# Last normalisation of a two-layer decoder trunk: block 0's second pass as a product with a scaled identity on TensorE, output rows stored in four halves

## The reference

```python
def layer_norm(x, g, b):
    xf = x.astype(jnp.float32)
    mu = jnp.mean(xf, axis=-1, keepdims=True)
    var = jnp.mean(jnp.square(xf - mu), axis=-1, keepdims=True)
    return ((xf - mu) * lax.rsqrt(var + LN_EPS) * g + b).astype(x.dtype)

def reference(...):
    h = layer_norm(x, ln_in_g, ln_in_b)
    for l in range(DEPTH):                      # DEPTH = 2
        mix = hybrid_mixer(h, ...)              # input projection, attention, gating, convolution, output projection
        h = layer_norm(DEEPNORM_ALPHA * h + mix, ln_mix_g[l], ln_mix_b[l])
        ffn = grouped_moe(h, ...)               # 16 experts, top 2 of one group of 4
        h = layer_norm(DEEPNORM_ALPHA * h + ffn, ln_ffn_g[l], ln_ffn_b[l])
    return h
```

## Time and profile before

| what | value |
|---|---|
| median of three runs | 640.27 us |
| the profiled execution | 642.03 us |
| its span, first to last instruction | 640.3 us |
| mean granted TensorE clock | 0.996 of full speed |
| busy share: PE, DVE, ACT, POOL | 97%, 47%, 33%, 23% |
| data moved | 246.70 MB, mean 385 GB/s |

### The profile page before, as it was taken

How to read it: one execution, slowest core, us unless ns; L and a number is a source line. 1 busy time by engine, 2 the same in 40 slices (tenths; PEclk the granted TensorE clock), 3 DMA queues, 4 the chain that set the end, 5 groups by cost and what they waited for, 6 DMA issues and landing times.

```text
span 640.3 us, 8170 instructions
## 1 busy us (share of the span) xinstructions
PE 618.4 (97%) x3239; PEld 335.2 (52%) x3239; DVE 298.5 (47%) x619; ACT 208.1 (33%) x465; POOL 148.7 (23%) x139
## 2 busy tenths in 40 slices
PE   9999999999999999997999999999999999999993
PEld 5887887534344344342488878764344344344331
DVE  6898897122141231230578988851141231330326
ACT  5831963232032131130184368342032131131211
POOL 1999400440000000000049971007000000000000
PEclk9999999999999999999999999999999999999998
DMA  8999299999999999999999646999999999999991
GB/s 358 431 425 415 108 427 360 377 430 427 412 426 428 427 426 427 427 425 429 429 428 381 234 198 272 416 338 416 432 417 426 431 423 428 427 425 423 432 383 69
DMA packets 21785, 246.70 MB, mean 385 GB/s; under 512 B 3276, under 2 KB 3404, under 8 KB 6384
## 3 DMA queue, kind: packets, MB, share of 16 engines
q1 hardware_dynamic: 18576, 236.56, 88.5%
q10 hardware_dynamic: 1152, 5.77, 2.3%
q0 software_dynamic: 2016, 3.82, 1.6%
HBM read 246.51 MB, written 3.15 MB: 390 GB/s over the span
## 4 chain that ended last, share of the span: by engine, by line
PE 80%; DMA 11%; DVE 7%; issue 1%; ACT 1%; DVEq 0%
PE bank L765 28%; PE bank L790 15%; PE bank L651 13%; DMA ring<-in_units 11%; PE bank L816 4%; PE bank L625 4%; PE bank L871 2%; DVE w_split L1470 2%; PE bank L883 2%; PE bank L731 2%; PE bank L698 1%; PE bank L639 1%; PE bank L777 1%; PE bank L953 1%; PE bank L579 1%
## 5 line engine op out<-in xcount | busy, mean ns | idle before, releaser
L765 PE MATMUL bank<-ring,xe_pair 128*64 128x512 f32 x976 | 213.3, 593 | 5.7 <-DMA ring<-in_units 5.7
L765 PEld LDWEIGHTS bank<-ring,xe_pair 128*64 128x64 f32 x976 | 71.3, 137 | 145.0 <-issue 134.0
L790 PE MATMUL bank<-ring,area_b 128*64 128x512 f32 x480 | 107.0, 596 | 1.6 <-DVE area_b L1693 1.6
L1691 DVE TENSOR_TENSOR area_b<-area_b,bank 128x512 f32<-128x512 f32 x16 | 11.0, 688 | 205.9 <-PE bank L765 205.9
L1326 POOL DMA_INDIRECT rows<-normal_rows,tiny_i x14 | 14.4, 1026 | 267.6 <-DVE tiny_i L1643 240.4
L1310 POOL TENSOR_TENSOR in_lo<-ring,in_hi 128x512 fp32r<-128x512 f32 x56 | 72.0, 1334 | 12.2 <-ACT in_hi L1081 12.2
L1158 ACT ACTIVATE area_b<-bank 128x512 f32<-128x512 f32 x16 | 9.6, 597 | 187.3 <-PE bank L765 187.3
L790 PEld LDWEIGHTS bank<-ring,area_b 128*64 128x64 f32 x480 | 32.9, 137 | 66.9 <-issue 59.0
L1136 ACT ACTIVATE xe_pair<-bank,small 128x128 f32<-128x128 f32 x128 | 47.0, 466 | 45.9 <-PE bank L731 35.6
L1277 POOL TENSOR_TENSOR rstd<-var_eps,tiny 128x1 f32<-128x1 f32 x18 | 10.6, 594 | 191.8 <-DVE var_eps L1402 191.8
L1712 DVE SCALAR_TENSOR_TENSOR y_lo<-bank,tiny,y_hi 128x512 fp32r<-128x512 f32 x32 | 24.0, 750 | 59.7 <-ACT y_hi L1171 59.7
(11 more groups left out here) (206 smaller groups left out, 789.4 us busy)
## 6 DMA issues: line engine op xcount, KB each, us to landing
ring<-in_units SPq DMA_DIRECT2D x101, 2048.0 KB, 19.5
ring<-in_units SPq DMA_DIRECT2D x8, 1024.0 KB, 23.0
ln_par<-in_ln_rows ACTq DMA_DIRECT2D x4, 1024.0 KB, 10.5
extra<-in_units SPq DMA_DIRECT2D x2, 2048.0 KB, 13.8
extra<-in_units SPq DMA_DIRECT2D x2, 1536.0 KB, 19.9
expert_half<-in_units SPq DMA_DIRECT2D x2, 1024.0 KB, 8.6
normal_rows<-mix SPq DMA_DIRECT2D x4, 512.0 KB, 8.8
h<-in_x SPq DMA_DIRECT2D x2, 512.0 KB, 4.1
```

What stands on the lines that cost most here:

```text
L765: mm = pe.matmul(bank[2 + m][e * SLOTS:(e + 1) * SLOTS, :], x[:, k, at + e * SLOTS:at + (e + 1) * SLOTS], w[c][:, m, e, :], start=k == 0, ...
L790: mm = pe.matmul(bank[5 + n][e * SLOTS:(e + 1) * SLOTS, :], hidT[:, k, e * SLOTS:(e + 1) * SLOTS], w[:, k, e, :], start=k == 0, stop=k == ...
```

## The change

The second pass of block 0 leaves VectorE. ScalarE makes a 128x128 diagonal matrix, the identity scaled row by row with block 0's `rstd` (`scaled_ident`, in memory that is free by then). TensorE forms, for each half, identity times the shift rows plus that diagonal times the half of the first pass, in banks 5 and 6, in float32. ScalarE copies each bank to `h`, and the copy is what SP waits for. VectorE makes block 0's first pass in two halves and tells TensorE of each; its work on block 1 is as before. SP now stores four halves, in the order block 0 first half, block 1 first half, block 0 second half, block 1 second half. Three semaphores get new names because they now serve both ends (`input_ready` is `rows_centred`, `conv_out` is `rows_out`, `proj_pe` is `block_product`). Of the diff, the places that only rename are left out.

```diff
+        scaled_ident = nc.alloc_sbuf_tensor_at("scaled_ident", [P, P], F32, offset=xT_at)
...
-            sp.wait_ge(result_ready, 1)
-            sp.dma_start(out[0, 0:P, :], h[:, 0, :]).then_inc(out_done, 16)
             for n in range(2):
                 half = slice(n * BANK, (n + 1) * BANK)
-                sp.wait_ge(result_ready, n + 2)
+                sp.wait_ge(rows_out, DEPTH + n + 1)
+                sp.dma_start(out[0, 0:P, half], h[:, 0, half]).then_inc(out_done, 16)
+                sp.wait_ge(result_ready, n + 1)
                 sp.dma_start(out[0, P:2 * P, half], h[:, 1, half]).then_inc(out_done, 16)
-            sp.wait_ge(out_done, 16 * 3)
+            sp.wait_ge(out_done, 16 * 4)
...
+            def result_products():
+
+                pe.wait_ge(par_in, 16 * (2 * DEPTH + 1))
+                for n in range(2):
+                    pe.matmul(bank[5 + n][:, :], ident, ln_par[:, 1, n * BANK:(n + 1) * BANK], start=True, stop=False)
+                pe.wait_ge(rows_kept, TB * DEPTH + 1)
+                for n in range(2):
+                    pe.wait_ge(rows_centred, 2 * TB * DEPTH + n + 1)
+                    pe.matmul(bank[5 + n][:, :], scaled_ident[:, :], h[:, 0, n * BANK:(n + 1) * BANK], start=False, stop=True)\
+                      .then_inc(block_product, 1)
+
             def layers_from(l):
 
                 n = layer(l)
                 if l == DEPTH - 1:
                     with pe.If(n > SLOTS):
                         more_rounds(l)
+                    result_products()
                     return
...
+            last = TB + DEPTH * LN_TILES - TB
+            act.wait_ge(ln_rstd, last + 1)
+            act.activation(scaled_ident[:, :], ident, ACT.Copy, scale=rstd[:, last:last + 1]).then_inc(rows_kept, 1)
+            for n in range(2):
+                act.wait_ge(block_product, DEPTH + n + 1)
+                act.activation(h[:, 0, n * BANK:(n + 1) * BANK], bank[5 + n][:, :], ACT.Copy).then_inc(rows_out, 1)
...
                 else:
+                    dve.wait_ge(par_in, 16 * (2 * l + 3))
+                    for n in range(2):
+                        half = slice(n * BANK, (n + 1) * BANK)
+                        dve.wait_ge(rows_kept, TB * l + n)
+                        dve.scalar_tensor_tensor(out=h[:, 0, half], in0=acc[:, 0, half], scalar=mv[:, 0, 0:1],
+                                                 in1=ln_par[:, 0, half], op0=ALU.subtract, op1=ALU.mult)\
+                           .then_inc(rows_centred, 1)
                     dve.wait_ge(rows_kept, TB * (l + 1))
-                    dve.wait_ge(par_in, 16 * (2 * l + 3))
-                    norm_apply(norm[0], acc[:, 0, :], h[:, 0, :], 0, ln_par[:, 0, :], ln_par[:, 1, :], result_ready)
                     step(dve.scalar_tensor_tensor(out=h[:, 1, :], in0=acc[:, 1, :], scalar=mv[:, 1, 0:1], in1=ln_par[:, 0, :],
                                                   op0=ALU.subtract, op1=ALU.mult))
```

More of the change, by code:

```diff
@@ L343, in trunk @@
         norm_ready = sem("norm_ready")
-        input_ready = sem("input_ready")
+        rows_centred = sem("rows_centred")
         h_ready = sem("h_ready")
@@ L359, in trunk @@
         conv_ln_done = sem("conv_ln_done")
-        conv_out = sem("conv_out")
+        rows_out = sem("rows_out")
         sg_out = sem("sg_out")
@@ L375, in trunk @@
         probT_dve = sem("probT_dve")
-        proj_pe = sem("proj_pe")
+        block_product = sem("block_product")
         xi_hi_ready = sem("xi_hi_ready")
@@ L575, in turn @@
                     if ready is not None:
-                        pe.wait_ge(input_ready, ready + half + 1)
+                        pe.wait_ge(rows_centred, ready + half + 1)
                     dst = bank[2 * b + half]
@@ L956, in layer @@
                 pe.wait_ge(sg_out, l + 1)
-                pe.wait_ge(conv_out, l + 1)
+                pe.wait_ge(rows_out, l + 1)
                 pe.wait_ge(v_ready, TB * (l + 1))
@@ L992, in layer @@
                     if b == 0:
-                        mm.then_inc(proj_pe, 1)
+                        mm.then_inc(block_product, 1)
                 pe.wait_ge(w_rt_scaled, l + 1)
@@ L1212, in _ @@
                 act.wait_ge(conv_ln_done, TB * (l + 1))
-                act.activation(mix[:, :, ATT + SG:D], mix[:, :, ATT + SG:D], ACT.Silu).then_inc(conv_out, 1)
+                act.activation(mix[:, :, ATT + SG:D], mix[:, :, ATT + SG:D], ACT.Silu).then_inc(rows_out, 1)
                 for qb in range(TB):
@@ L1424, in input_center @@
                     dve.tensor_scalar(normal[:, b, at], src[:, at], mv[:, b, 0:1], rstd[:, i:i + 1], ALU.subtract, ALU.mult)\
-                       .then_inc(input_ready, 1)
+                       .then_inc(rows_centred, 1)
             def layer_norms(src, dst, gain, shift, width, signal):
@@ L1822, in _ @@
                         residual(l, (i - KC - 2) // 2, 0)
-                dve.wait_ge(proj_pe, l + 1)
+                dve.wait_ge(block_product, l + 1)
                 step(residual(l, 0, 1))
```

## The result

Over 13 runs of each, the changed kernel's median is 643.87 us and that of the kernel before 640.69 us; the ratio is 1.0046, interval 1.0033 to 1.0058, which is 3 us. The profiled execution took 643.51 us against 642.03. I had forecast 640.7 us, range 639.2 to 642.3.

A forecast was written before the change was run, and what follows sets the result against it. The tail was taken as bound by VectorE's four passes in a row, then a store's two microseconds. Branch stall and TensorE's work offset VectorE's saving; queued stores add 0.4 us: 640.27 + 0.4 = 640.7 us, range 639.2 to 642.3.

The forecast's parts named there:

- TensorE's exit: TensorE's second branch, behind the products to the end: put at nothing; 0.4 us if begun only with the last product's end.
- My first rival: TensorE's branch ahead of the new products is cheap, about 0.1 us: 639.4 us; chance 17 in 100.
- my second rival: Granted clock falls under TensorE's new products, steps twice as long: 643.8 us, or 642.2 if later; 11 in 100.
- The choice of the branch's price: TensorE's last branch ahead of the new products: the upper price, 3577 ns, taken over some 0.1 us.
- VectorE's part: VectorE's tail without block 0's second pass: block 1 early by 1.38 us.
- the scaled identity: ScalarE's 128x128 diagonal, begun at 632.53: takes 0.37 us, ready at 632.9, before TensorE needs it.
- the shift products: TensorE's first new products, right behind the last branch: 632.95 to 634.9 or so.
- The stores: SP's four stores: 0.34 us each to issue, queueing at 0.6 us per 256 KB; +0.4 us at the end.

The follow-up runs named there:

- e5: Changed kernel with the four result products once, at the end of TensorE's program, so no second jump follows them; ratio 1.0017.
- e6: Changed kernel with the result products once at the program's end and 12 small products keeping TensorE busy ahead of the branch; ratio 1.0007.
- e1: Changed kernel with 12 small bf16 products on TensorE ahead of its last branch, to keep it busy in the stall; ratio 1.0038.
- e4: Kernel before with one wait added, so TensorE's last branch waits until block 0's result is ready; ratio 1.0016.
- e2: Changed kernel with the result products on the fall-through side of TensorE's last branch, a second copy behind the further rounds; ratio 1.0040.
- e11: Changed kernel with 40 small products (80 instructions) in place of the last layer's further rounds; one execution, 642.31 us.
- e3: Changed kernel with SP storing block 1's halves first and block 0's halves after; ratio 1.0022.
- e12: Changed kernel with 110 small products (220 instructions) in place of the last layer's further rounds; one execution, 643.59 us.
- e7: Changed kernel with result products once at the program's end, small products ahead of the branch, and block 1's halves stored first; ratio 0.9995.
- e9: Changed kernel with the shift products ahead of TensorE's last branch and the diagonal products once at the program's end; ratio 0.9994.

## Why the prediction was wrong, step by step

**The step that failed** is TensorE's exit: "I put it at nothing". I had priced it only as a wait of TensorE's own, against the barrier, and in that it was right: the branch ends at 636.2, five microseconds early. But the jump has two transfers of 16 KB, and the second, about 4.8 us behind the branch's start, falls among the stores and, as I read the single packets behind them, holds up one transfer engine's share. The profile had shown both code blocks; in the kernel before they passed while no store was under way, and I didn't ask what they would meet once moved. Without the second jump the changed kernel goes from 1.0046 to 1.0017 (e5), 1.9 us less; at the 640.69 us of the kernel before that is 641.8 us, inside my range. By tails it is 1.0 us for e5 against the changed kernel and 1.5 us for e6 against e1; e4 shows such a price, 1.2 us, with TensorE doing no work at all. My first rival had the same gap: e2 and e11 have the cheap branch, and the exit takes their gain.

**The clock**, my second rival with 11 in 100, was the case in the profiled execution. I had argued that at 632.9 TensorE works again; the fall came in spite of that. The whole of it is 1.7 us in the products (four steps longer by 0.43 us), but at the end it is worth 0.6 us or less where the late code transfer follows (0.6 us of tail, changed kernel against e1; 0.3 us between the changed kernel's own executions), and 1.1 us of tail or 1.4 us between executions where it doesn't (e5). The fall stands in the profiles of the changed kernel, e3 and e5, and not in that of e12 with the same idleness, so that the idle time alone doesn't decide it; what does is open. I gave the rival 643.8 us if the clock fell for all products. That this is near the measured 643.87 is luck: it fell for half of them, and five executions without the fall took just as long.

**The choice of the branch's price** was right: 3732 ns against the 3577 that I took, and e12 shows that the near target made no difference. By the Trainium skill, Runtime: NRT & Kernel Launch, section Instruction fetch mechanics, a taken branch whose target is outside the current two-page window has to wait for a fetch; the long jumps agree (3577 and 3732 ns). Its 2048 instructions for TensorE do not fit: over 220 the jump took 3627 ns. By my estimate of 256 instructions to a block, 220 on is at most the next block, so e12 speaks against the window too if the next block is meant to be in it; the runs don't show which blocks were there.

**VectorE's part** (1.38 us forecast) measured 1.29; the scaled identity took 401 ns where I had put 370; the shift products began 0.1 us later than forecast. **The stores** were right in kind: four close ones queue. Behind one another their issues took 0.43 to 0.46 us, not 0.34. With stall, clock and exit as forecast, e6 fits the sum of these terms by its ratio (0.4 us), less well by its tail (1.0 us).

**The sum** of the 3 us, by the runs, one thing taken away after the other: the second jump (e5), the clock (e6), the order of the stores that the late copies made bad (e7). By the ratios these are 1.9, 0.6 and 0.8 us, each give or take about 1.1 us by their intervals, so that only the first is clear of nothing; by the tails of the profiled executions, where the clock had fallen in the changed kernel and in e5, they are 1.0, 1.1 and 1.0 us. (The branch took 3344 ns in e5 and 3875 ns in e6, so the tails show the clock's share too small and the order's too large.) The three overlap, as e1 and e2 show by gaining little each while the others stand. What remains, 7.8 us, is the tail of the kernel before, its freed 1.3 us used up by the stall and the crowding of the stores (e9, without the stall, gets 0.6 us of them back).

## What to carry to other kernels

Work put behind a branch on an engine that had none there pays for the branch: read the branch's own row, not only the instructions, and ask for each jump what its code transfers will meet. Put what doesn't depend on the branch ahead of it, and the rest where no second jump follows. And when a waiting pass moves to another engine, weigh first what leaving it out would bring: here 1.0 us, less than the exit alone cost by the ratios.

## What the runs showed of the hardware

- A taken branch on TensorE cost 239 ns over 80 instructions and 3.3 to 4.2 us over 220 and more, where one not taken cost 64 to 89 ns. On ScalarE and VectorE, over 38 to 67 instructions, 45 to 55 ns.
- Code blocks of 16 KB that pass among the last stores delayed them. With four close stores of 256 KB the last landing took 4.6 us (e1), against 2.8 us in the same kernel without the second jump (e6); with three stores and no other change it took 3.3 us against 2.1 (e4). In e1 what was late were eight packets of 2 KB, one at a time, which I read as the share of a single transfer engine.
- With four close stores of 256 KB and no code block among them, SP's wait ended 4.1 to 4.2 us after the first one's issue (e5, e6, e7, e9).
- After full load TensorE was idle for 2.2 to 2.5 us in four of the profiled executions. In one (e12) the granted clock stayed at 1.00 until the products were done. In the others it fell to 0.50: 1.4 us after TensorE had begun to work again (changed kernel), 0.9 us after (e5), and 0.2 us before (e3).
